# A decoder step on one core: sample query rows by a store and a broadcast load, state outputs with 32 stationary columns, branch tiles ahead of the head sums

## What is computed

```python
aq, af, ai, ag, bq, bk, bv, gate_a, gate_b = split(h @ w_in)     # 1024 -> 5632 columns
# branch a, HGRN2: 4 heads, state S (128 x 128) for each sample and head
S_new = f * S + outer(k, v);   o = q @ S_new
o_a = rmsnorm(o, g_norm) * silu(ag)
# branch b, differential attention: 4 heads, two maps of 64
s = q . k * 64 ** -0.5 - slope * distance      # samples: 256 cached keys in 2 pages, and their own
o_b = rmsnorm((softmax(s0) - lam * softmax(s1)) @ v) * 0.8
merged = sigmoid(gate_a) * (o_a @ w_proj_a) + sigmoid(gate_b) * (o_b @ w_proj_b)
x = x + gt1 * rmsnorm(merged @ w_out)
# then a mixture of experts: top 4 of 32, w_gate_up (1024 x 2048) and w_down (1024 x 1024) each
```

## Time and profile before

| | |
|---|---|
| times | 1348.39 us median of 3 (1341.27, 1348.39, 1360.29) |
| the profiled execution | 1343.04 us, span 1341.4 us |
| busy | TensorE 1156.7 us (86%), weight loads 494.6, VectorE 526.4 (39%), ScalarE 263.5, GpSimd 66.0 |
| HBM read / written | 478.00 MB / 5.76 MB, 361 GB/s over the span |

### The profile page before, as it was taken

The page is one execution under the profiler, slowest core; times in us unless marked ns, Lnnn a source line. Parts: engine busy times, 40 slices in busy tenths (PEclk is TensorE's granted clock), DMA queues, the critical chain, the costliest instruction groups (busy, mean ns, idle before and its releaser), DMA issues.

```text
span 1341.4 us, 21833 instructions
## 1 busy us (share of the span) xinstructions
PE 1156.7 (86%) x8778; PEld 494.6 (37%) x8778; DVE 526.4 (39%) x868; ACT 263.5 (20%) x469; POOL 66.0 (5%) x127
## 2 busy tenths in 40 slices
PE   4999999999969669798797997999966997668996
PEld 1766676776523113232122332333311332112332
DVE  1534744332644224344243442444522443222544
ACT  3002410130402112122121221222211221111222
POOL 1200102120120000000000000000000000000000
PEclk9999999989959879999798998999998998878998
DMA  9966785446579999999999999799999999999994
GB/s 330 312 251 229 275 286 182 152 174 236 224 279 428 427 428 428 427 429 426 427 428 428 427 427 428 298 409 407 409 428 426 428 428 428 427 427 428 428 428 168
DMA packets 65564, 484.75 MB, mean 361 GB/s; under 512 B 5853, under 2 KB 28754, under 8 KB 37690
## 3 DMA queue, kind: packets, MB, share of 16 engines
q1 hardware_dynamic: 58272, 462.10, 83.5%
q0 software_dynamic: 6096, 18.16, 4.2%
q10 hardware_dynamic: 1130, 3.52, 0.7%
HBM read 478.00 MB, written 5.76 MB: 361 GB/s over the span
## 4 chain that ended last, share of the span: by engine, by line
PE 53%; DMA 36%; DVE 9%; issue 1%; ACT 0%; POOL 0%; SPq 0%; DVEq 0%; POOLq 0%; ACTq 0%
DMA big<-in_w_gate_up 24%; PE PB L1018 17%; PE PB L617 9%; PE PB L1041 8%; DMA big<-in_w_down 8%; PE PB L571 2%; PE PB L873 2%; PE PB L634 2%; DVE mod L1814 2%; PE PB L897 2%; DMA big<-in_w_mod 2%; DVE mod L1808 1%; DVE mod L1811 1%; DVE mod L1807 1%; PE PB L993 1%; PE PB L585 1%
## 5 line engine op out<-in xcount | busy, mean ns | idle before, releaser
L1018 PE MATMUL PB<-big,cst 128*32 128x512 f32 x3072 | 394.4, 660 | 116.9 <-DMA big<-in_w_gate_up 116.9
L1018 PEld LDWEIGHTS PB<-big,cst 128*32 128x32 f32 x3072 | 99.1, 116 | 386.8 <-issue 203.7
L1807 DVE TENSOR_SCALAR mod<-PB 64x512 f32<-64x512 f32 x48 | 32.8, 683 | 479.7 <-PE PB L1018 479.7
L1041 PE MATMUL PB<-big,cst 128*32 128x512 f32 x1536 | 176.3, 596 | 7.2 <-DMA big<-in_w_down 7.1
L617 PE MATMUL PB<-hTG,big 128*128 128x264 f32 x576 | 140.0, 399 | 2.7 <-DVE hTG L1297 2.2
L617 PEld LDWEIGHTS PB<-hTG,big 128*128 128x128 f32 x576 | 110.1, 196 | 32.0 <-issue 11.1
L1244 ACT ACTIVATE mod<-mod 64x512 f32<-64x512 f32 x48 | 30.3, 631 | 464.5 <-DVE mod L1807 464.5
L985 PE MATMUL PB<-tok,att 64*128 64x512 f32 x392 | 97.4, 615 | 0.0
L1818 DVE TENSOR_REDUCE att<-hTG 128x272 f32<-128x1088 f32 x48 | 61.7, 1286 | 81.0 <-PE PB L993 81.0
L1041 PEld LDWEIGHTS PB<-big,cst 128*32 128x32 f32 x1536 | 44.2, 109 | 116.2 <-issue 78.8
L973 PE MATMUL PB<-wide,att 128*32 128x256 f32 x1176 | 81.2, 410 | 0.0
(11 more groups left out here) (295 smaller groups left out, 927.6 us busy)
## 6 DMA issues: line engine op xcount, KB each, us to landing
big<-in_w_gate_up SPq DMA_DIRECT2D x128, 2048.0 KB, 26.5
big<-in_w_down SPq DMA_DIRECT2D x64, 2048.0 KB, 22.0
big<-in_w_mod SPq DMA_DIRECT2D x24, 1024.0 KB, 8.4
big<-in_w_in SPq DMA_DIRECT2D x22, 1024.0 KB, 7.5
wide<-in_cache_k POOLq DMA_DIRECT2D x16, 256.0 KB, 6.6
hTG<-in_cache_v POOLq DMA_DIRECT2D x16, 256.0 KB, 4.0
big<-in_w_out SPq DMA_DIRECT2D x4, 1024.0 KB, 7.6
big<-in_state_hgrn POOLq DMA_DIRECT2D x4, 512.0 KB, 7.6
```

The source lines that it names most:

```text
L1018: mm = pe.matmul(GU[32 * j:32 * j + 32, :], mo["xT"][:, r * P + u * M:r * P + (u + 1) * M], w[:, r * 2 * D + j * 512:r * 2 * D + (j + 1) * ...
L1041: mm = pe.matmul(DN[32 * j:32 * j + 32, :], mo["actT"][:, r * 64 + u * M:r * 64 + (u + 1) * M], w[:, r * D + half * 512:r * D + (half + 1) ...
L1807: dve.tensor_scalar(mo["glu"], GU[0:64, :], LIMIT, None, ALU.min).then_inc(S("glu_ready"), 1)
```

## The change

- The queries of the samples are stored as 8 rows into a DRAM tensor `q_rows`, and one load reads all 8 rows into each of the 128 partitions (`q_all`, 2 MB, over the place of `SA` and `S0`). Both are issued by GpSimd. `query_rows` and its eight banks are gone, and `query(b)` reads `q_all`. The small copies `vbs` and `vbT` come ahead of `query(0)` on VectorE, and the first loads of `S0` wait for all eight queries.
- `out_sample(h)` has the queries as stationary operand: a tile of 32 columns for each sample and head that is zero but for one column (`queries`, made by VectorE with a memset and a copy), and the 128 columns of the state move. The samples go through the four column groups, two for each. A new step, `state_outputs`, sums the four groups and turns the result, as `sample_outputs` does for the values. VectorE copies PB[4] once more for it.
- `head_sums("a")` comes after the first two branch tiles, and `OA` is finished ahead of the `logit_consts` sums.
- The load of `G` waits for the state outputs, since `queries` lies there.

```diff
@@ AUX_ORDER: qb0 to qb7 are gone, "so" is new between mt2 and lc @@
 def aux(name):
-    return PB[5 + AUX[name] % 3]
+    return PB[5 + (AUX[name] + 1) % 3]
@@ GpSimd @@
-            for b in range(NS):
-                if b >= 2:
-                    pool.wait_ge(S("k_used"), b - 1)
+            for b in range(2):
+                pages(b, kpg, "cache_k", "k")
+            pool.wait_ge(S("tok_ready"), 1)
+            pool.dma_start(q_rows[:, :], qs_rows[0:NS, :]).then_inc(S("rows_stored"), 16)
+            pool.wait_ge(S("rows_stored"), 16)
+            src = bass.AP(q_rows.tensor, 0, [[0, P], [1, NS * W]])
+            pool.dma_start(q_all[:, :, :], src).then_inc(S("q_loaded"), 16)
+            for b in range(2, NS):
+                pool.wait_ge(S("k_used"), b - 1)
                 pages(b, kpg, "cache_k", "k")
             for b in range(2):
                 pages(b, vpg, "cache_v", "v")
+            pool.wait_ge(S("k_used"), NS)
             for h in range(2):
                 pool.dma_start(S0[:, h, :, :], st_in[h]).then_inc(S(f"s0_{h}_loaded"), 16)
...
-            pool.wait_ge(S("v_used"), NS // 2)
-            pool.wait_ge(S("g_stored"), 128)
+            pool.wait_ge(S("osa_used"), H)
+            pool.wait_ge(S("rows_stored"), 144)
@@ TensorE @@
             def out_sample(h):
-                pe.wait_ge(S("vals_ready"), 1)
+                pe.wait_ge(S("spread_ready"), 1)
                 pe.wait_ge(S("s0_ready"), h + 1)
                 for b in range(NS):
-                    mm = pe.matmul(PB[4][:, h * NS + b:h * NS + b + 1], S0[:, h % 2, b, :],
-                                   AQ[:, h, TP + b:TP + b + 1], start=True, stop=True)
+                    j = b % 4
+                    mm = pe.matmul(PB[4][32 * j:32 * j + 32, h * P:(h + 1) * P], queries[:, b, h, :], S0[:, h % 2, b, :],
+                                   start=(b < 4), stop=(b >= 4))
...
-            def query_rows(b):
-                bank = begin(f"qb{b}")
-                pe.wait_ge(S("aux_free"), AUX["qs"] + 1)
-                full(pe.matmul(bank[:, :], ident[0:NS, b:b + 1].to_broadcast([NS, P]), qs_rows[0:NS, :],
-                               start=True, stop=True))
...
+            def state_outputs():
+                bank = begin("so")
+                pe.wait_ge(S("vals_ready"), 2)
+                for h in range(H):
+                    mm = pe.matmul(bank[:, h * NS:(h + 1) * NS], vals[:, h * P:(h + 1) * P],
+                                   C("onehot_e")[:, 0:NS], start=True, stop=True)
+                full(mm)
...
-            in_T(10, [(out_sample, 2), (outer, 3)], [(mod_cols, "mt2", 2)], [(out_sample, 3)], [(logit_consts,)])
-            head_sums("a", ETf)
+            in_T(10, [(out_sample, 2), (outer, 3)], [(mod_cols, "mt2", 2)], [(out_sample, 3)], [(state_outputs,), (logit_consts,)])
             def branch(name, src, first):
                 for s in range(KC):
+                    if first + s == 2:
+                        head_sums("a", ETf)
@@ VectorE @@
             def query(b):
-                q = bank(f"qb{b}")
+                q = q_all[:, b, :]
+                dve.wait_ge(S("q_loaded"), 16)
                 dve.wait_ge(S(f"k{b % 2}_loaded"), 32 * (b // 2 + 1))
...
+            rows_out("vbs", vbs[:, :], "vbs_ready")
+            rows_out("vbT", sv("vbT"))
             for b in range(4):
                 query(b)
-            rows_out("vbs", vbs[:, :], "vbs_ready")
-            rows_out("vbT", sv("vbT"))
...
             copy(vals, PB[4][:, :], "vals_ready")
+            do(dve.memset(queries, 0.0))
+            copy(own_queries, AQ[:, :, TP:T].rearrange("p h b -> p b h"), "spread_ready")
...
+            dve.wait_ge(S("osa_used"), H)
+            copy(vals, PB[4][:, :], "vals_ready")
+            b = bank("so")
+            copy(OA[:, :, TP:T], b[:, 0:H * NS].rearrange("p (h b) -> p h b", h=H))
+            free()
+            dve.nop().then_inc(S("oa_ready"), 1)
             b = bank("lc")
...
-            dve.wait_ge(S("osa_used"), H)
-            copy(OA[:, :, TP:T], PB[4][:, 0:H * NS].rearrange("p (h b) -> p h b", h=H))
-            dve.nop().then_inc(S("oa_ready"), 1)
```

More of the change, by code:

```diff
@@ L125 @@
 AUX_ORDER = ["vt"] + [f"xt{k}" for k in range(KC)] + ["mt0"] + """
-    qs tok0 tok1 toks qb0 qb1 qb2 qb3 vbs vbT sc00 sc01 sc10 sc11 sc20 sc21 sc30 sc31
-    pt0 pt1 qb4 pt2 qb5 pt3 qb6 ob0 qb7 ob1 ss ob2 ob3 kt0 kt1 pd as0 as1
-    kv0 vas kv1 kks kv2 ou00 ou01 kv3 mt1 ou10 ou11 oa0 oa1 sv oa2 oa3 ou20 ou21 nb0 nb1 nb2 ou30 ou31 mt2 lc
+    qs tok0 tok1 toks vbs vbT sc00 sc01 sc10 sc11 sc20 sc21 sc30 sc31
+    pt0 pt1 pt2 pt3 ob0 ob1 ss ob2 ob3 kt0 kt1 pd as0 as1
+    kv0 vas kv1 kks kv2 ou00 ou01 kv3 mt1 ou10 ou11 oa0 oa1 sv oa2 oa3 ou20 ou21 nb0 nb1 nb2 ou30 ou31 mt2 so lc
     na0 na1 na2""".split()
@@ L199, in build @@
         x_spill = nc.dram_tensor("x_spill", (T, D), F32, kind="Internal").ap()
+        q_rows = nc.dram_tensor("q_rows", (NS, W), F32, kind="Internal").ap()
         g_rows = nc.dram_tensor("g_rows", (4, 9, D), F32, kind="Internal").ap()
@@ L217, in build @@
         S0 = late[:, base + 2048:base + 4096].rearrange("p (s b v) -> p s b v", s=2, b=NS)
+        q_all = late[:, base:base + 4096].rearrange("p (b n) -> p b n", b=NS)
         QT = late[:, base + 4096:base + 4096 + H * T].rearrange("p (h t) -> p h t", h=H)
@@ L245, in build @@
         vpg = G[:, :, :].rearrange("p s (g n) -> p s g n", g=NPG)
+        Gf = hTG[:, KC * T:KC * T + 2 * D]
+        queries = Gf[:, 0:1024].rearrange("p (b h m) -> p b h m", b=NS, h=H)
+        own_queries = Gf[:, 0:NS * 129].rearrange("p (b x) -> p b x", b=NS)[:, :, 0:128].rearrange(
+            "p b (h m) -> p b h m", h=H)[:, :, :, 0]
         gaT = gates[:, 0:KC * T].rearrange("p (s t) -> p s t", s=KC)
@@ L499, in _ @@
                     pool.dma_start(g_rows[which, :, i * 512:(i + 1) * 512],
-                                   mod[32 * j:32 * j + 9, g, :]).then_inc(S("g_stored"), 16)
-            pool.wait_ge(S("v_used"), NS // 2)
-            pool.wait_ge(S("g_stored"), 128)
+                                   mod[32 * j:32 * j + 9, g, :]).then_inc(S("rows_stored"), 16)
+            pool.wait_ge(S("osa_used"), H)
+            pool.wait_ge(S("rows_stored"), 144)
             pool.dma_start(G[:, 0, :], bass.AP(g_rows.tensor, 0, [[0, P], [1, D]])).then_inc(S("g1_loaded"), 16)
@@ L843, in _ @@
                    [(rows_from, "tok1", KT_, slice(P, 2 * P), P)],
-                   [(rows_from, "toks", KT_, slice(TP, T), NS), (query_rows, 0)],
-                   [(query_rows, 1)], [(query_rows, 2)])
-            in_T(0, [(query_rows, 3), (value_rows, "vbs"), (value_cols, "vbT")], [(scores, 0, 0)], [(scores, 0, 1)], [(scores, 1, 0)])
+                   [(rows_from, "toks", KT_, slice(TP, T), NS)],
+                   [], [])
+            in_T(0, [(value_rows, "vbs"), (value_cols, "vbT")], [(scores, 0, 0)], [(scores, 0, 1)], [(scores, 1, 0)])
             in_T(1, [(scores, 1, 1)], [(scores, 2, 0)], [(scores, 2, 1)], [(scores, 3, 0)])
-            in_tok(2, [(scores, 3, 1)], [(probs_T, 0)], [(probs_T, 1)], [(query_rows, 4)], [(probs_T, 2)],
-                   [(query_rows, 5)])
-            in_T(3, [(probs_T, 3), (query_rows, 6)], [(out_b, 0), (query_rows, 7)], [(out_b, 1), (sample_scores,)],
+            in_tok(2, [(scores, 3, 1)], [(probs_T, 0)], [(probs_T, 1)], [], [(probs_T, 2)],
+                   [])
+            in_T(3, [(probs_T, 3)], [(out_b, 0)], [(out_b, 1), (sample_scores,)],
                  [(out_b, 2), (out_b, 3)])
@@ L1128, in _ @@
             for c in range(2):
-                act.wait_ge(S("tok_ready"), c + 1)
+                act.wait_ge(S("tok_ready"), c + 2)
                 act.dma_start(kout[c], krows[c]).then_inc(S("tok_stored"), 16)
-            act.wait_ge(S("tok_ready"), 3)
+            act.wait_ge(S("tok_ready"), 4)
             act.dma_start(o[5][0, :, 0].rearrange("b h n -> b (h n)"), krows[2]).then_inc(S("tok_stored"), 16)
@@ L1201, in x1T_copy @@
                 act.nop().then_inc(S("aux_free"), 1)
-            act.wait_ge(S("g_stored"), 128)
+            act.wait_ge(S("rows_stored"), 144)
             for step, c in enumerate(CHUNKS):
@@ L1401, in query @@
             def query(b):
-                q = bank(f"qb{b}")
+                q = q_all[:, b, :]
+                dve.wait_ge(S("q_loaded"), 16)
                 dve.wait_ge(S(f"k{b % 2}_loaded"), 32 * (b // 2 + 1))
-                tt(prod, kpg[:, b % 2, :, :], q[:, :].unsqueeze(1).to_broadcast([P, NPG, W]), ALU.mult)
-                free()
+                tt(prod, kpg[:, b % 2, :, :], q.unsqueeze(1).to_broadcast([P, NPG, W]), ALU.mult)
                 do(dve.tensor_reduce(sS[:, :, 8 * b:8 * b + 8], prod.rearrange("p g (r d) -> p g r d", d=64),
@@ L1445, in out_a @@
                 free()
-            rows_out("qs", qs_rows[0:NS, :])
+            rows_out("qs", qs_rows[0:NS, :], "tok_ready")
             rows_out("tok0", krows[0], "tok_ready")
```

## The result

The changed kernel took 1336.09 us (median; 1332.61 to 1343.48, 20 runs), the kernel before, on the same chips, 1349.17 (1341.27 to 1360.29, 20 runs). The ratio is 0.9919 with a 95% interval of 0.99 to 0.9938: 11 us faster by the ratio, 13 by the medians, and less than 2% either way. The forecast was 1332 us and a gain of 14.4 us, the range 1316 to 1347.

A forecast was written before the change was run, and what follows sets the result against it. TensorE was taken to bound the mixer, the weights' rate the experts behind it. 6.5 + 4.1 - 0.9 + 2.2 + 2.5 = 14.4 us gave 1328.6 from the profiled run, 1334.0 from the median; forecast 1332 us, range 1316 to 1347.

The forecast's parts named there:

- Query rows: Eight `query_rows` leave TensorE, 8.4 us; with the old wait at `sample_scores`, 6.5 us gained.
- the wait at this place grows to 3 us: At `sample_scores`, TensorE waits 3 us for VectorE, where it waited 1.15, as sample 6's pages come late.
- holds ... a piece of `w_in`: Stated way to be wrong: the 2 MB load holds VectorE or a piece of `w_in`; no size given.
- rival 1: Little but the instruction count: clock falls as before or elsewhere, VectorE late at `sc11` and `sample_scores`; gain 9, 1338 us; chance 0.2.
- The load: The 2 MB load of query rows lands between 86 and 98 us, VectorE asks at 93.6; no cost taken.
- rival 4: Queries late: VectorE stands at `query(0)` until `q_loaded`; against the change from 111 us on; 1358 us at 25 beyond; chance 0.04.
- `sc11`: Fourth score matmul, 112.8 us instead of 117.03; `query(3)` ends at 108 to 111.3; cost 0, up to 1 us.
- State outputs: Four `out_sample` calls at 0.7 us each instead of 1.68 to 1.78: gain 4.1 (2.9 to 5.1); `state_outputs` costs 0.9.
- Head sums: Two branch tiles and logit sums cover TensorE's idle 2.23 us before the head sums: 2.2 gained; branch a's norm delays nothing.
- The clock: TensorE's clock: a term of 2.5 us in the summed gain.
- rival 2: Everything comes: pages after 5.6 us, clock up 4.5; gain 20 us, 1327 us; chance 0.15.
- The profile's own signs: Expected after: `query(0)` at 93 to 94 us, `sample_scores` near 169, `out_sample` 0.5 to 1.0, last branch tile 307 to 308.

The follow-up runs named there:

- after_again: The changed kernel as it is, run and profiled again: 1335.18 us (8 runs), 0.991 of the kernel before.
- before_b: The kernel before, unchanged, profiled once more: 1348.69 us (one run).
- q_twice: The changed kernel with the 2 MB broadcast load done twice in a row, `query(0)` waiting for the second: 1343.57 us (one run).
- experiment 1: Each part put alone into the kernel before: query rows 1344.18 us, state outputs 1339.07, head sums 1345.02; also the changed kernel again, 1335.18.
- so_only: The kernel before with only the state outputs part, `OA` copied ahead of the logit sums, `head_sums` unmoved: 1339.07 us, 0.9927 of before.
- experiment 2: On TensorE's wait for the fourth pair's value pages: kernel before reprofiled, 1348.69 us; changed kernel with last `w_in` piece held, 1328.93, or state stores held, 1342.65.
- best: The changed kernel with first value pages behind the last query, `query(4)` earlier, last `w_in` piece held for the value pages: 1327.43 us, 0.9834 of before.
- vq: The changed kernel with first value pages behind the last query and `query(4)` ahead of head 3's scores: 1331.18 us, 0.9884 of before.
- q4_early: The changed kernel with only `query(4)` moved ahead of the scores of head 3 on VectorE: 1333.90 us (one run).
- hs_only: The kernel before with only the head sums behind two branch tiles and `OA` copied ahead of the logit constants: 1345.02 us, 0.9964 of before.
- w_hold: The changed kernel with the last piece of `w_in` held on SyncE until the value pages have landed: 1328.93 us (one run).

## Why the prediction was right, and where it wasn't

Time, sign and range held. By its own steps, each against the stretches of several profiles (the timed parts are coarser):

- **Query rows, predicted 6.5, measured 4.3.** The stretch to `sample_scores` is 108.1, 109.0, 108.51 and 109.79 us in the four profiles without the part (mean 108.85), and 103.65 to 105.19 in the five with it and no other edit there (mean 104.53). The 8.4 us of matmuls are gone. The step that failed is "the wait at this place grows to 3 us": it took VectorE for the last to come, from the earlier trace rows, and never asked what TensorE's own tile needs. VectorE came about when the prediction said (175.6 us, on its clock 168.4), and in after TensorE doesn't wait for it. With TensorE some us earlier, a piece of `w_in` is last, 4.0 to 4.9 us, and the tile that uses it is slow, by 1.5 us in after, 1.7 in after_again and up to 2.4 in the other profiles. 8.4 and the old wait of 1.15 less these are 4.0 and 3.2 in the first two; before also had up to 0.8 us of waiting at `sc00` for VectorE (before_b, at 103.34 us), gone in after. The text named this as a way to be wrong ("holds ... a piece of `w_in`"), but for the 2 MB load in the front, and gave it no price. It is rival 1's mechanism, late data, at another place. The prediction did say that the DMA engines are as full there as before, and used it only for the key pages.
- **The load, predicted 0, measured 0.** It landed 7.8 us after its issue, at 91.0; on the prediction's clock that is 83.8, two us ahead of the 86 to 98 given, since the store went out at 73.1 on that clock and landed in 2.6 us, not in the 3.5 to 8.3 of the earlier trace rows. Nothing on VectorE waited for it. The Trainium skill's rule ("DMA: Bandwidth & Descriptors", Anatomy of one DMA) had given 6.8 us for the load and 2 for the store; the trace has 7.8 and, for the store, 2.6 to its landing and 2.86 to the next issue. The zero was right by a narrow margin, though: another 2 MB cost 4 to 5 us (q_twice). The prediction had measured the margin in latency only (rival 4's 14 us of delay), not in bytes.
- **`sc11`, predicted just in time.** `query(3)` ended at 118.5 us in the profile of after, whose start is 7.2 us later than that of before: 111.3 on the prediction's clock, the late end of its 108 to 111.3. `sc11` started at 120.18 without a wait. Right.
- **State outputs, predicted 4.1 and -0.9.** 0.57 us a call where 0.7 was taken, against 1.68 to 1.78 before: 4.6 us, inside the 2.9 to 5.1 given. The last call waits 0.91 us for VectorE, for which the prediction had taken 0.7 off its clock term, so 3.7 net. `state_outputs` cost 0.79. Nothing shows a price of the column groups between full tiles.
- **Head sums, predicted 2.2.** The idle 2.23 us are gone, and the norm of branch a holds nobody. Right; experiment 1 adds that with `OA` copied earlier the move of the head sums wasn't needed for it (so_only).
- **The clock, predicted 2.5, measured about 5.** The slow tiles at 252 and 270 us (5.49 and 5.42 us in before) take 3.83 in after: 3.3 us. In the last stretch, 4.0 us shorter, 2.2 are the idle time and 1.1 the head sums (2.83 to 1.77), the rest the first tiles. The falls at 254, 270 and 292 us are gone, as in rival 2; the fall at 222 us was not of that kind but one that comes and goes (experiment 2). Half of what was in reach was too careful, and made up for what the query part lacked: that part gave 4.3 for 6.5, the other parts, predicted at 7.9 us together, gave 9.8. That the sum came out near is luck.

The stretches sum to 4.3 + 5.8 + 4.0 = 14.1 us; the timed runs say 11 to 13. By its interval the ratio of after allows 8.4 to 13.5 us, so a little is missing. The middle stretch of after and after_again is 0.3 to 1.2 us longer than before_b's, and the start and the wait of experiment 2 may come in their long form more often with the change. No run tested either. The profile's own signs fit so far: `query(0)` at 101.23 is 94.0 on the prediction's clock, where 93 to 94 stood. But `sample_scores` is at 171.6 on it and not near 169, and the last branch tile ends at 320.7 us, in after_again at 315.9, where 307 to 308 stood: the wait in the middle and the piece of `w_in`, and in after the late start, make most of the difference.

What the prediction could not have read from its one profile is that this execution was a short one: its page gave 1341.4 us of span, the low end of the kernel's runs. It saw that (the median lay 5.4 us above) and set the forecast between the two. One cause, a wait of 2.6 us with a slow tile behind it, shows only in a second profile.

## What to carry to other kernels

When a step is taken from the engine that bounds a stretch, list for the next thing it does every operand with its own deadline, the streamed weights too, and move each deadline by the gain: here 8.4 us were taken, and a weight piece, not the helper engine, took half of them back. Where the DMA engines are full, order transfers by when they are wanted: holding back one 1 MB load that nobody needed yet, asking for 1 MB of value pages later and for a pair of key pages earlier (`query(4)`) gave some 9 us more, beside the 11 to 13 of the change. Profile a kernel twice before forecasting by tenths of a per cent. Gains of parts that cure the same stall are not added.

## What the runs showed of the hardware that was not expected

- Waits of 1.9 to 4.9 us for a DMA cost more than themselves: the next full tile took 5.3 to 6.7 us in place of 3.8 (mean granted clock 0.75 and 0.59 in those windows of after). Behind waits of 0.2 to 1.1 us it took 3.83 (best, vq, q4_early). Not every wait of that length does it: behind 2.22 us for VectorE at 36 us in before the tiles ran at 3.6 us each (96 instructions in 21.60 us).
- With a 1 MB load issued on one queue 0.8 to 0.9 us ahead of the last 256 KB page of another, TensorE waited 1.9 to 3.2 us for that page (ten profiles); with the load 0.3 to 0.5 us behind it, or held, it didn't wait (before, hs_only, w_hold, best).
- The first products with `w_mod` take 1.07 or 1.93 us for eight, from execution to execution of the same program (after and after_again). The granted clock in the window from 21 to 36 us is 1.00 in both, so the profile doesn't say why, and no run tried it.
- One row of 16 KB read by 128 partitions, 2 MB in SBUF, came in 7.8 us beside a running weight stream; 16 grouped matmuls with 32 stationary and 128 moving columns took 0.57 us between full tiles.
